# Low parts of streamed weights: a second, accumulating load in place of GpSimd's subtraction, in a one-core hybrid encoder block

## The reference, cut to what matters

```python
x = x + 0.5 * swiglu(rmsnorm(x, ffn1_norm), ffn1_w_gu, ffn1_w_down)
x = x + token_mixing(rmsnorm(x, mix_norm), w_in, ...)          # ends in @ w_out
x = x + cross_attention(rmsnorm(x, xa_norm), rmsnorm(mem, mem_norm), xa_wq, xa_wkv, xa_wo)
x = x + 0.5 * swiglu(rmsnorm(x, ffn2_norm), ffn2_w_gu, ffn2_w_down)
return rmsnorm(x, final_norm)
```

## Time and profile before

| what | value |
|---|---|
| median of 3 runs | 1164.62 us (1162.81 to 1164.76) |
| the profiled execution's own time | 1163.28 us |
| span of the profile, first to last instruction | 1161.5 us |
| busy: TensorE, ScalarE, VectorE, GpSimd | 1141.4, 432.2, 465.8, 548.4 us |
| GpSimd's subtractions (L349), 400 halves | 548.2 us |
| ScalarE's copies to `wh` (L360, L373), 200 | 211.4 us |
| moved by DMA | 113.10 MB, 97 GB/s over the span |

### The profile page before, as it was taken

How to read it: one execution, slowest core, us unless ns; L and a number is a source line. 1 busy time by engine, 2 the same in 40 slices (tenths; PEclk the granted TensorE clock), 3 DMA queues, 4 the chain that set the end, 5 groups by cost and what they waited for, 6 DMA issues and landing times.

```text
span 1161.5 us, 14979 instructions
## 1 busy us (share of the span) xinstructions
PE 1141.4 (98%) x5382; PEld 951.1 (82%) x5382; DVE 465.8 (40%) x662; ACT 432.2 (37%) x586; POOL 548.4 (47%) x404
## 2 busy tenths in 40 slices
PE   9999999999999999999999999999999999999997
PEld 7888888888887888887878888788888888888886
DVE  6432322322223667877567223454322322321112
ACT  6423223222223545553246543344222222222222
POOL 0745445455554433333326873155545445455550
PEclk9999999999999999999999999999999999999999
DMA  7332232233223222111222542122332232233312
GB/s 230 127 108 90 90 108 90 90 109 109 99 100 108 73 73 74 64 66 64 79 91 91 182 163 73 37 74 93 107 108 90 90 108 90 90 109 109 107 57 73
DMA packets 36965, 113.10 MB, mean 97 GB/s; under 512 B 3776, under 2 KB 10048, under 8 KB 36800
## 3 DMA queue, kind: packets, MB, share of 16 engines
q1 hardware_dynamic: 35728, 111.00, 28.7%
q10 hardware_dynamic: 1200, 1.57, 0.4%
HBM read 110.47 MB, written 2.10 MB: 97 GB/s over the span
## 4 chain that ended last, share of the span: by engine, by line
issue 39%; PE 33%; POOL 26%; POOLq 0%; DVE 0%; ACT 0%; DVEq 0%
POOL wl L349 26%; PE bank L1007 11%; PE bank L1008 11%; PE bank L1009 11%; POOLq L347 0%; POOLq L345 0%; DVE x L994 0%; PE n_bank L1050 0%; PE o_bank L1155 0%; DVEq L100 0%; ACT rstd L612 0%; DVE x L987 0%; PE n_bank L1153 0%; PE n_bank L1155 0%; ACT rstd L613 0%
## 5 line engine op out<-in xcount | busy, mean ns | idle before, releaser
L349 POOL TENSOR_TENSOR wl<-raw,wh 128x512 fp32r<-128x512 f32 x400 | 548.2, 1394 | 587.5 <-ACT wh L360 320.4
L1007 PE MATMUL bank<-xh,wh 128*128 128x512 f32 x936 | 369.6, 395 | 0.0
L1009 PE MATMUL bank<-xh,wl 128*128 128x512 f32 x936 | 364.8, 390 | 0.0
L1008 PE MATMUL bank<-xl,wh 128*128 128x512 f32 x936 | 364.7, 390 | 0.0
L373 ACT ACTIVATE wh<-raw 128x1024 fp32r<-128x1024 f32 x104 | 110.3, 1061 | 391.9 <-DVE ubuf L700 218.6
L1007 PEld LDWEIGHTS bank<-xh,wh 128*128 128x128 f32 x936 | 176.0, 188 | 38.4 <-issue 1.9
L1008 PEld LDWEIGHTS bank<-xl,wh 128*128 128x128 f32 x936 | 176.1, 188 | 37.5 <-issue 1.7
L1009 PEld LDWEIGHTS bank<-xh,wl 128*128 128x128 f32 x936 | 175.9, 188 | 37.0
L360 ACT ACTIVATE wh<-raw 128x1024 fp32r<-128x1024 f32 x96 | 101.1, 1053 | 131.2 <-PE bank L1009 130.5
L1007 PE MATMUL bank<-hid_h,wh 128*128 128x512 f32 (+1 forms) x374 | 141.0, 377 | 0.0
L1009 PE MATMUL bank<-hid_h,wl 128*128 128x512 f32 (+1 forms) x374 | 140.8, 377 | 0.0
(11 more groups left out here) (216 smaller groups left out, 1097.2 us busy)
## 6 DMA issues: line engine op xcount, KB each, us to landing
raw<-w_all SPq DMA_DIRECT2D x200, 512.0 KB, 3.3
x<-x_t SPq DMA_DIRECT2D x8, 256.0 KB, 6.1
out_t<-x SPq DMA_DIRECT2D x8, 256.0 KB, 2.5
raw<-w_all SPq DMA_DIRECT2D x6, 256.0 KB, 6.2
memf<-mem_t ACTq DMA_DIRECT2D x1, 1024.0 KB, 4.9
raw<-w_all ACTq DMA_DIRECT2D x2, 256.0 KB, 4.3
gbuf<-masks_d SPq DMA_DIRECT2D x1, 256.0 KB, 6.2
ident<-ident_d SPq DMA_DIRECT2D x1, 64.0 KB, 5.8
```

The source lines that it names most:

```text
L349: ins = nc.gpsimd.tensor_tensor(wl[:, c, half], raw[:, c, half], wh[:, c, half].bitcast(f32), SUB)
L1007: nc.tensor.matmul(out_, a[0], b_[0], start=first, stop=False)
L1008: nc.tensor.matmul(out_, a[0], b_[1], start=False, stop=False)
L1009: return nc.tensor.matmul(out_, a[1], b_[0], start=False, stop=last)
```

## The change

ScalarE writes the negative of the high part into `wl` (a rounding copy with scale -1) before it writes `wh`. GpSimd no longer subtracts. It issues, for each unit from 4 on, a DMA that reads the unit's weights from HBM a second time and adds them onto `wl` in SBUF, so that `wl` holds raw minus high part. SyncE's load of the next `raw` waits for `hi_ready` rather than for `lo_ready`. TensorE waits for `hi_ready` and for the landing of the accumulating load (`lo_added`, one semaphore for each slot). The first four units are made as before.

```diff
@@ SyncE
-            with sp.Fori(1, NU // SLOTS) as i:
+            sp.wait_ge(lo_ready, SLOTS)
+            for c in range(SLOTS):
+                sp.dma_start(raw[:, c, :], w_all[SLOTS + c, :, :]).then_inc(raw_loaded[c], 16)
+            with sp.Fori(2, NU // SLOTS) as i:
                 for c in range(SLOTS):
-                    sp.wait_ge(lo_ready, i * SLOTS + (c - SLOTS + 1))
+                    sp.wait_ge(hi_ready, i * SLOTS + (c + 1 - SLOTS))
@@ GpSimd
-            with pool.Fori(1, NU // SLOTS) as i:
-                for c in range(SLOTS):
-                    pool.wait_ge(hi_ready, i * SLOTS + (c + 1))
-                    for half in (slice(0, UNIT // 2), slice(UNIT // 2, UNIT)):
-                        ins = nc.gpsimd.tensor_tensor(wl[:, c, half], raw[:, c, half], wh[:, c, half].bitcast(f32), SUB)
-                    ins.then_inc(lo_ready, 1)
+            for u in range(SLOTS, NU):
+                pool.wait_ge(minus_ready, u + 1 - SLOTS)
+                pool.dma_start(wl[:, u % SLOTS, :], w_all[u, :, :], accum_op=ADD).then_inc(lo_added[u % SLOTS], 16)
@@ ScalarE, in hi and in ahead_loop
+                nc.scalar.activation(wl[:, slot, :], raw[:, slot, :], ACT.Copy, scale=-1.0).then_inc(minus_ready, 1)
                 nc.scalar.activation(wh[:, slot, :], raw[:, slot, :], ACT.Copy).then_inc(hi_ready, 1)
@@ TensorE
+            def lo_wait(u, off=None):
+                if off is not None:
+                    pe.wait_ge(lo_added[u % SLOTS], off + 16 * (u // SLOTS))
+                elif u < SLOTS:
+                    pe.wait_ge(lo_ready, SLOTS)
+                else:
+                    pe.wait_ge(hi_ready, u + 1)
+                    pe.wait_ge(lo_added[u % SLOTS], 16 * (u // SLOTS))
...
-                pe.wait_ge(lo_ready, ou + (u + 1))
+                if off_u is not None:
+                    pe.wait_ge(hi_ready, ou + (u + 1))
+                lo_wait(u, off_lo)
```

More of the change, by code:

```diff
@@ L199, in block_kernel @@
         lo_ready = sem("lo_ready")
+        minus_ready = sem("minus_ready")
+        lo_added = [sem(f"lo_added{i}") for i in range(SLOTS)]
         unit_used = sem("unit_used")
@@ L1012, in wpair, with group @@
                 return wh[:, slot, lo:hi_], wl[:, slot, lo:hi_]
-            def group(u, g, off_u=None, off_g=None, x_phase=None, src=(xh, xl), cols_=T, ready=None):
+            def lo_wait(u, off=None):
[6 more added lines that the diff above has]
+                    pe.wait_ge(lo_added[u % SLOTS], 16 * (u // SLOTS))
+            def group(u, g, off_u=None, off_g=None, off_lo=None, x_phase=None, src=(xh, xl), cols_=T, ready=None):
                 ou = 0 if off_u is None else off_u
@@ L1086, in ffn @@
                         for c in range(2):
-                            pe.wait_ge(lo_ready, u0 + c + 1)
+                            lo_wait(u0 + c)
                             pe.wait_ge(group_read, g0 + c + 1)
@@ L1099, in ffn @@
                     for c in range(4):
-                        group(u0 + c, g0 + c, i * 4, i * 4)
+                        group(u0 + c, g0 + c, i * 4, i * 4, i * 16)
                 ud, gd, nd = u0 + N_UP, g0 + N_UP, len(DOWN_SPLIT)
@@ L1108, in down @@
                         u = ud + m * nd + c
-                        pe.wait_ge(lo_ready, (0 if i is None else i * (4 * nd)) + (u + 1))
+                        if i is not None:
+                            pe.wait_ge(hi_ready, i * (4 * nd) + (u + 1))
+                        lo_wait(u, None if i is None else i * (16 * nd))
                         for k in range(n):
@@ L1133, in ffn @@
                         if h == 0:
-                            pe.wait_ge(lo_ready, u + 1)
+                            lo_wait(u)
                         for k in range(n):
```

## The result

The changed kernel takes 1188.76 us (median of 4 runs, 1185.88 to 1191.58) against 1163.71 for the kernel before, a ratio of 1.0218 (95% interval 1.0184 to 1.0251): slower by 25 us, where 1195 us was forecast. The profiled execution took 1190.50 us; its span is 1188.7, 27.2 us longer than before. The total came out as forecast. The places were partly wrong, and the errors cancelled, as the rest shows.

The account below looks back on a forecast made before the run. TensorE was taken to bound the kernel. Start 4.2, keys and `vx` 24.4 and unit 132 3.9, less 2 for VectorE's relief, gave +30.5 us, so 1193.8 for the profiled execution and a median of 1195 us, range 1168 to 1255.

Parts of the forecast that it names:

- The bound: Whole kernel: TensorE, busy 1141.4 of 1161.5 us, sets the time; POOL's removed 548 us give nothing but 2.5 us of waits.
- The price of an accumulate: DMA engines: an accumulating load costs twice a plain one, 3.14 us per unit (bounds 1.57 and 4.71), both loads 4.71.
- The landing: Every streamed unit: the low part lands 7.0 us after the negative copy ends (bounds 3.3 and about 10).
- Start and unit 132: Units 4 and 132: the low part lands after TensorE wants it, +4.2 us and +3.9 us.
- The half-clock stretch: After TensorE gaps of some 2 us: each new one can add 1.7 us; a widening of other cases, not its own.
- `w_out`: First unit after `together`: some +3 us, swallowed by TensorE's existing wait at unit 104, so nothing of its own.
- Keys and `vx`: Units 104 to 121: two loads need 4.71 us per unit, more than TensorE; last landing 710.6, +24.4 us.
- The mixer: VectorE's chain there runs faster without POOL's subtraction, less ScalarE's extra copies: -2 us, bounds -5.6 and +2.
- The relief: Rival: the accumulate lands within 3.6 us and VectorE's gain in the mixer outweighs, about 1160 us; chance 0.08.
- The DMA engines: Rival: they become the bound throughout if an accumulate costs over 3.42 us (down), 3.87 (up); 1215 us and up; chance 0.25.
- Latency alone: Rival: the accumulate costs about as little as a plain load, only late landings cost; 1171 us, range 1168 to 1183; chance 0.25.

Follow-up runs that it names:

- experiments 4 and 5: 4: kernel before, GpSimd subtracting 2 x 8 of 1024 columns, 1148.06 us; 5: accumulating load only for units 72 to 98, 1157.58 us, also 101 to 103, 1156.73 us.
- the six that choose by ACC: Changed kernel with a list ACC choosing per unit between accumulating load and GpSimd's subtraction; six different lists, 1156.73 to 1182.55 us.

## Why the prediction was right, and where it was not

**The bound.** Right: TensorE sets the time, and in both feed-forward layers nothing changed (+0.1 us), with 165 units loaded twice too. Where the first units are made by subtraction, the losses behind unit 5 (+6.5) are the start's, not the steady layer's.

**The price of an accumulate.** Twice a plain load, 3.14 us, was taken; the packets' busy time was 2.97 us against 1.57 for a plain load from the same queue. The factor is 1.9. The Trainium skill ("Collectives: The Full Stack", the section on the bandwidth ceiling) has a factor of two from two source reads; the measured factor agrees, and no run here shows the reads themselves. The estimate of 2.1 us from its rate is under the 2.97 us of the packets, but near what an accumulating load adds to a plain one where the engines are full, 3.8 - 1.57 = 2.3 us (see the keys).

**The landing.** Right: 7.0 us after the end of the negative copy at unit 4, 6.1 and 6.2 at units 99 and 132.

**Start and unit 132.** The waits were right (4.2 and 3.5 us against 4.2 and 3.9 forecast). The half-clock stretch was named as a widening and left out of the sum; each of the long gaps brought one, worth 1.3 (unit 99) to 2.9 us (unit 4) beyond the gap. Measured +7.1 and +5.8.

**`w_out`.** This step failed. It counted only unit 100, as swallowed by unit 104's wait. Unit 99 comes at the head of `together` and lost 4.7; unit 100 lost 5.7 with its clock stretch, and 3.6 + 1.1 of these were won back at 101 to 104 (1.7 of the 3.6 by the missing stretch at the lower clock). The stage costs +5.7 up to and with unit 104, for which nothing was put down.

**Keys and `vx`.** The mechanism was right for the keys (a wait before nearly every one, the DMA engines at a share of 1.05) and the size was off: +24.4 forecast. The term of 17 x 4.71 us added the two loads' busy times. In the saturated window the engines moved 274 GB/s for 28 us, 7.67 MB, so a pair of loads (1.049 MB) took 3.8 us: busy times of packets on two queues of one engine overlap, and the share can pass 1. The landings on the trace's semaphores say the same: the low parts of units 105 to 115 landed from 637.96 to 676.71, 3.9 us apart. At 3.8 us the 17 steps come to 65 in place of 80. Measured from the first key to the last `vx` matmul: +11.1 us. Unit 104's low part was not late at all: it landed at 631.7, and TensorE started on the unit at 635.2, 8 us later than before. 6.9 of the stage's loss are at unit 117 alone, a gap of 4.4 us with its clock stretch behind, and there a short cover adds to the engines' load: TensorE used unit 113, whose slot it takes, until 676.3, only three `vx` units of 2.8 us stood between, and its low part landed at 688.9. The prediction priced this place by the rate alone.

**The mixer.** -4.7, 1.7 of it the clock, with -2 put down and -5.6 as the bound. The relief of VectorE is shown by experiments 4 and 5; what ScalarE's copies take from it is not separated from the clock.

**The sum.** 4.2 + 24.4 + 3.9 - 2 = 30.5 was forecast; 7.1 - 2.1 (start) - 4.7 + 9.3 (96 to 103) + 9.4 (104 to 121) + 2.3 + 5.8 + 0.1 = 27.2 was measured. The key stage was taken 15 us too high, the start, `w_out` and unit 132 with their clock 12 too low, the mixer 3 too high, and units 122 to 131 (+2.3) were not in it. The -2.1 of the start isn't the change at all. That the total comes within 6.2 us is luck: two errors of over 10 us stand against each other.

**Rivals.** The DMA engines were no bound in the steady stages: 0.90 in the down projection, as 94% had been worked out. Latency alone is what the kernel without the add comes near: 1165.75 us where 1171 was given for it. The relief is real, 4.2 us in the mixer and 5.4 in the time with only its units changed, and decides where nothing else is exposed.

## What to carry to other kernels

An operation moved off an engine with time to spare onto a longer path costs nothing where a slot's cover (the time from its coming free to its use) is long, and its full delay where several buffers come free together or short units stand between: list for every unit how long before its use its slot comes free, not for every stage, and apply the change unit by unit. If a fix relieves one exposed unit, the next one in line loses its cover. Before stages of two executions are compared, take out the stretches at the lower clock that only one of them has. Two queues' busy times can't be added to a bound; take the bytes per second of a saturated window.

## What the runs showed of the hardware

**An accumulating load.** 2.97 us of 16 engines' packet time per 512 KB against 1.71 with conversion alone and 1.57 plain; beside a plain load, with the engines full, 3.8 us for the pair. Issue to landing in the mixer's input units (72 to 98, median) is 5.8 us in the changed kernel and 6.6 in the six that choose by ACC; why is open. POOL spends 868 ns to issue one and 530 ns for either of the others.

**The clock after a gap.** In the changed kernel the gaps of 3.6 to 4.7 us were followed by 3.4 to 6.8 us at the lower level, the gaps of 1.0 to 1.5 us in the keys by none. In the kernel before gaps of 1.8 and 2.2 us were followed by 3.4 us at the lower level. It isn't the gap alone: at the same place in the mixer TensorE has a gap of 2.1 us in the changed kernel, in the one without the add and in eight of the other experiments; only the one without the add falls to the lower level behind it. Windows of the one without the add, before and behind that gap:

```profile
470.00:477.00 7.00, 5.26 (x29) 4.25 (x28) 5.55 (x14) 4.76 (x6) 0.53 (x1) 1.00 0.31 94
477.00:487.00 10.00, 10.00 (x39) 9.13 (x39) 5.82 (x16) 7.60 (x10) 0.53 (x1) 0.50 0.42 145
```

And of the changed kernel:

```profile
475.00:481.00 6.00, 4.26 (x25) 3.41 (x24) 5.06 (x14) 3.78 (x5) 0.86 (x1) 1.00 0.31 49
481.00:491.00 10.00, 10.00 (x67) 9.04 (x66) 6.61 (x17) 8.13 (x11) 0.86 (x1) 1.00 0.70 179
```

Ten microseconds at half clock, 39 matmuls in place of 67, in one and none in the other. That is why the mixer's relief is missing in that profile. What decides it stays open.

**A count in POOL's queue.** Across the four kernels with 178 or more accumulating loads, the 61st, 114th, 118th and 175th of them started 1.0, 1.6, 1.0 and 1.0 us after the end of ScalarE's copy, where 0.3 is usual, at whatever time they came; in the kernel with 165 the first three of these did too. In the changed kernel the 114th is unit 117, so 1.3 us of its gap may be this. In the kernel without the add the 114th and 115th were late (3.0 and 1.6 us after the copy). The cause stays open.
